# Norms before seven FFNs finished in two halves of the tokens

## What is computed

```python
def rmsnorm(x, g):
    y = xf * lax.rsqrt(jnp.mean(xf * xf, axis=-1, keepdims=True) + NORM_EPS)
    return y.astype(x.dtype) * g

def modulate(h, g, shift, scale):
    return rmsnorm(h, g) * (1 + scale) + shift

def swiglu(y, w_gu, w_down):
    gate, up = jnp.split(y @ w_gu, 2, axis=-1)
    return (jax.nn.silu(gate) * up) @ w_down

def half_ffn(h, m, off, g, w_gu, w_down):
    y = modulate(h, g, m[off], m[off + 1])
    return h + 0.5 * m[off + 2] * swiglu(y, w_gu, w_down)

...
        x = deepnorm_residual(x, f, g1, ln_g[l, 0], ln_b[l, 0], 0.5)
        u = modulate_2(x, sh2, sc2)
```

## Time and profile before

| | us |
|---|---|
| median of 3 runs | 3207.75 (3206.51 to 3209.87) |
| the profiled execution, its own time | 3206.11 |
| its span, first to last instruction | 3204.3 |
| TensorE busy | 2980.6 (93%) |
| VectorE busy | 1899.3 (59%) |
| ScalarE busy | 568.7 (18%) |
| mean granted clock of TensorE | 0.97 of full |

### The profile page before, as it was taken

How to read it: one execution, slowest core, us unless ns; L and a number is a source line. 1 busy time by engine, 2 the same in 40 slices (tenths; PEclk the granted TensorE clock), 3 DMA queues, 4 the chain that set the end, 5 groups by cost and what they waited for, 6 DMA issues and landing times.

```text
span 3204.3 us, 61066 instructions
## 1 busy us (share of the span) xinstructions
PE 2980.6 (93%) x26800; PEld 2554.4 (80%) x26800; DVE 1899.3 (59%) x3378; ACT 568.7 (18%) x1289; POOL 224.4 (7%) x363
## 2 busy tenths in 40 slices
PE   7999999977988899999989999989999989989898
PEld 6444444776777699999879999977889989967898
DVE  1777666643555487686647767745326656633674
ACT  1000001443343100100231010024111020031201
POOL 0000000431342000000000000000000000000000
PEclk8999999999999899999999999999999999998999
DMA  5668986101300456466325656633335535522452
GB/s 225 235 236 314 370 336 229 66 4 56 105 4 4 171 191 234 163 228 217 126 99 175 214 180 202 212 106 112 125 112 170 176 119 181 173 69 71 132 191 94
DMA packets 365794, 514.86 MB, mean 161 GB/s; under 512 B 11536, under 2 KB 344400, under 8 KB 357984
## 3 DMA queue, kind: packets, MB, share of 16 engines
q1 hardware_dynamic: 347824, 364.11, 34.9%
q0 software_dynamic: 17136, 144.19, 11.6%
q10 hardware_dynamic: 576, 2.75, 0.2%
HBM read 509.97 MB, written 1.05 MB: 159 GB/s over the span
## 4 chain that ended last, share of the span: by engine, by line
PE 83%; DVE 5%; DMA 5%; ACT 4%; issue 2%; POOL 1%; SPq 0%; DVEq 0%; ACTq 0%; POOLq 0%
PE PS L2487 28%; PE PS L2527 15%; PE PS L2417 7%; PE PS L588 5%; PE PS L2437 5%; PE PS L608 5%; PE PS L761 3%; PE PS L1658 2%; PE PS L1583 2%; DMA ADAW<-in_ada_rows 2%; PE PS L2538 2%; PE PS L2396 2%; DMA W<-in_ffn_w_down 1%; DVE ADAW L2723 1%; PE PS L1436 1%
## 5 line engine op out<-in xcount | busy, mean ns | idle before, releaser
L2487 PE MATMUL PS<-Y,W 128*128 128x128 f32 x4928 | 594.4, 280 | 43.4 <-ACT Y L2640 32.1
L2487 PEld LDWEIGHTS PS<-Y,W 128*128 128x128 f32 x4928 | 578.1, 196 | 48.8 <-issue 34.5
L2487 PE MATMUL PS<-Y,ARENA 128*128 128x128 f32 x3696 | 438.6, 275 | 0.0
L2487 PEld LDWEIGHTS PS<-Y,ARENA 128*128 128x128 f32 x3696 | 425.9, 192 | 0.0
L2417 PE MATMUL PS<-Y,W 128*128 128x512 f32 x704 | 304.6, 596 | 2.2 <-DVE Y L2945 2.2
L2527 PE MATMUL PS<-ARENA,W 128*128 128x128 f32 x2464 | 286.5, 275 | 7.8 <-DVE ARENA L2829 5.0
L2527 PEld LDWEIGHTS PS<-ARENA,W 128*128 128x128 f32 x2464 | 280.1, 192 | 9.7 <-DVE ARENA L2829 6.7
L2417 PEld LDWEIGHTS PS<-Y,W 128*128 128x128 f32 x704 | 134.5, 191 | 171.6 <-issue 171.1
L2723 DVE SCALAR_TENSOR_TENSOR ADAW<-ADAW,CB 128x1024 f32<-128x1024 f32 x200 | 238.6, 1221 | 29.4 <-DMA ADAW<-in_ada_rows 28.9
L608 PE MATMUL PS<-W 64*64 64x64 f32 x4608 | 116.4, 226 | 45.4 <-ACT W L858 24.5
L2437 PE MATMUL PS<-ARENA,W 128*128 128x512 f32 x352 | 154.2, 601 | 4.7 <-DVE ARENA L2777 4.7
(11 more groups left out here) (399 smaller groups left out, 3702.6 us busy)
## 6 DMA issues: line engine op xcount, KB each, us to landing
ADAW<-in_ada_rows POOLq DMA_DIRECT2D x52, 2048.0 KB, 8.8
W<-in_ffn_w_gu SPq DMA_DIRECT2D x88, 1024.0 KB, 8.0
W<-in_ffn_in SPq DMA_DIRECT2D x88, 1024.0 KB, 7.6
W<-in_ffn_w_down SPq DMA_DIRECT2D x32, 1408.0 KB, 11.2
W<-in_ffn_out SPq DMA_DIRECT2D x32, 1408.0 KB, 9.1
ADAW<-in_ada_rows POOLq DMA_DIRECT2D x64, 512.0 KB, 6.5
W<-in_even_w_in SPq DMA_DIRECT2D x40, 512.0 KB, 4.7
W<-in_e_w_in SPq DMA_DIRECT2D x22, 512.0 KB, 4.8
```

Source lines behind the costliest of these rows:

```text
L2487: last = mm(block_bank(b, q), w[left][:, k, q * P:(q + 1) * P], YB[right][:, k], start=(k == 0 and p not in (2, 5)), stop=(k == 3), skip_g ...
```

## The change

In the norms before the seven small FFNs (`by_half`), VectorE takes the reciprocal of tokens 0 to 127 alone, multiplies tiles 0 to 3 and then 4 to 7 of those tokens, and does the same with tokens 128 to 255. ScalarE scales and shifts 128 columns at a time, all eight tiles of the first half and then all eight of the second: sixteen steps for eight. `s_y` counts the first half alone, one for every second tile; a new semaphore `s_yh` counts the second half, one for every four tiles, and the token sums wait for that one.

```diff
@@ norm, deepnorm, program @@
-            add("rms", layer, 3 * k, T, n_rs, vec("norm_g", 24 * layer + 8 * k, 8), bump("y"), n["nx"])
+            add("rms", layer, 3 * k, T, n_rs, vec("norm_g", 24 * layer + 8 * k, 8), bump("y"), n["nx"], of is not None)
...
-            add("layer_norm", n_rs, g, b, then, bump("y") if then else None, n["nx"])
+            add("layer_norm", n_rs, g, b, then, bump("y") if then else None, n["nx"], of is not None)
...
@@ ScalarE @@
-            def modulated(src, layer, k, n_nx):
+            def modulated(src, layer, k, n_nx, by_half=False):
 
                 sh = MOD[:, layer, 8 * k:8 * (k + 1)] if k is not None else GS[:, 1]
+                if by_half:
+                    for h in range(2):
+                        t = slice(HT * h, HT * (h + 1))
+                        for j in range(DT):
+                            if j % 4 == 0:
+                                act.wait_ge(s_nx, n_nx - PIECES + 1 + 2 * h + j // 4)
+                            ins = A(Y[:, j, t], (Y[:, j, t] if k is not None else X[:, 0, j, t]), ACT.Identity,
+                                    bias=sh[:, j:j + 1], scale=GS[:, 0, j:j + 1])
+                            if h == 0 and j % 2 == 1:
+                                ins.then_inc(s_y, 1)
+                            if h == 1 and j % 4 == 3:
+                                ins.then_inc(s_yh, 1)
+                    return
...
@@ VectorE @@
             def token_sums(b, done, n_, n_y=None):
                 if n_y:
-                    dve.wait_ge(s_y, n_y - PIECES // 2)
+                    dve.wait_ge(s_yh, n_y - 1)
                 V.tensor_tensor(b["T1"], b["B12"], b["B11"], ALU.subtract).then_inc(done, 1)
                 dve.wait_ge(done, n_ + 1)
                 if n_y:
-                    dve.wait_ge(s_y, n_y)
+                    dve.wait_ge(s_yh, n_y)
...
-                        token_sums(YB, s_ty, 4 * i, n_y)
+                        token_sums(YB, s_ty, 4 * i, 2 * (i + 1))
...
+            def normed_by_half(dst, late=None):
+
+                for h in range(2):
+                    t = slice(HT * h, HT * (h + 1))
+                    link(V.reciprocal(RS[:, t], RS[:, t]))
+                    for i in (0, 4):
+                        if late and i:
+                            late(h)
+                        V.tensor_tensor(dst[:, i:i + 4, t], X[:, 0, i:i + 4, t],
+                                        RS[:, t].unsqueeze(1).to_broadcast([P, 4, HT]), ALU.mult).then_inc(s_nx, 1)
+
...
                 dve.wait_ge(s_rs, n_rs)
+                if by_half:
+                    normed_by_half(Y[:, :, 0:S])
+                    return
...
                 dve.wait_ge(s_rs, n_rs)
+                if by_half:
+                    normed_by_half(X[:, 0])
+                    return
```

More of the change, by code:

```diff
@@ L227, in build @@
         s_yl = sem("y_of_first_sequence_ready")
+        s_yh = sem("y_of_second_half_ready")
         s_nx = sem("normed_piece_ready")
@@ L2250, in program @@
             x_scales[bump("xa")] = (vec("final_g", 0, DT), None)
-            add("layer_norm", n_rs, vec("final_g", 0, DT), None, (2, 0), bump("y"), n["nx"])
+            add("layer_norm", n_rs, vec("final_g", 0, DT), None, (2, 0), bump("y"), n["nx"], True)
             if stop == 2:
@@ L2642, in modulated, with rms @@
                     ins.then_inc(s_y, 1)
-            def rms(layer, k, T, n_rs, g, n_y, n_nx):
+            def rms(layer, k, T, n_rs, g, n_y, n_nx, by_half):
                 if T > S:
@@ L2647, in rms, with layer_norm @@
                 else:
-                    modulated(slice(0, S), layer, k, n_nx)
-            def layer_norm(n_rs, g, b, then, n_y, n_nx):
+                    modulated(slice(0, S), layer, k, n_nx, by_half)
+            def layer_norm(n_rs, g, b, then, n_y, n_nx, by_half):
                 if then:
-                    modulated(slice(0, S), None, None, n_nx)
+                    modulated(slice(0, S), None, None, n_nx, by_half)
                     return
@@ L2929, in small_ffn, with first_rms @@
                 dve.wait_ge(s_ev, sec["t1"])
-            def first_rms(layer, k, T, n_rs, g, n_y, n_nx):
+            def first_rms(layer, k, T, n_rs, g, n_y, n_nx, by_half):
                 kt = DT // PIECES
```

## The result

| | before | after |
|---|---|---|
| median on the same chip, us | 3209.03 (3206.51 to 3214.56, 6 runs) | 3221.64 (3214.68 to 3228.41, 6 runs) |
| ratio to before, 95% interval | | 1.0039 (1.0024 to 1.0055) |
| profiled execution, own time | 3206.11 | 3221.04 |
| its span | 3204.3 | 3219.3 |
| mean granted clock | 0.97 | 0.968 |

The change makes the kernel slower, by 12.6 us in these runs. Repeated later without any edit beside 30 runs of before, it was slower by 9.8 us, ratio 1.0032 (1.0020 to 1.0044). The forecast was +9.9 and 3216.0; the 3221.64 of the first comparison lies 0.6 above the range.

A forecast was written before the change was run, and what follows sets the result against it. TensorE paces each small FFN from product 2 on, so its start and TensorE's clock count. Later product 2 (+4.1 us) and half clock (+5.8) add 9.9 to 3206.1, giving 3216.0 us, range 3208.5 to 3221.

The forecast's parts named there:

- Bound and path: Small FFN heads: product 2's start counts; product 1 comes 1.0 us sooner, off the path, as its copy follows sixteen ScalarE steps.
- ScalarE's spacing: Scale-and-shift before each small FFN: sixteen 128-column steps 0.39 us apart, 0.48 long, against eight 0.49 apart now.
- Product 2 later: Seven small FFN heads: product 2 at 8.50 us after the root's end, usually 8.15 now; +4.1 us in sum.
- Token sums: VectorE's T1 and T2 wait for the second half; 1.3 us of slack before product 6 asks, cost nothing.
- Clock: TensorE at half clock behind product 2: 1.4 us a norm, 9.8 over seven, less 4.0 now: +5.8 us (-4.0 to +7.2).
- The sum: Whole kernel: 4.1 for later product 2 plus 5.8 for half clock, +9.9 us on 3206.1, giving 3216.0.
- 1.4 for the spread: Allowance in the range's upper end of 3221 for the spread of the runs: 1.4 us.
- The clock costs what it does now: Rival: TensorE's low stretch is over by product 2, only the later copy costs: +4.1, 3210.2 us; chance 0.31.
- Cheap short steps: Rival: ScalarE's steps 0.30 us apart, product 2 up to 1.1 us sooner, total 3196 to 3200 us; chance 0.06.
- Nothing on the path: Rival: ScalarE's steps 0.36 us apart, product 2 not later, clock as now: 3206 to 3208 us; chance 0.06.

The follow-up runs named there:

- copy_dve: Changed kernel, with VectorE and not ScalarE copying product 1 in the first unit of each small FFN: 3204.32 us, ratio 0.9993 to before.
- warm_before: Kernel before the change, with 512-column matmuls nobody reads filling TensorE's pauses before products 1 and 2 of the seven norms: 3202.61 us, ratio 0.9986.
- warm_wide: Changed kernel, with 512-column matmuls nobody reads filling TensorE's pauses before products 1 and 2 in all seven norms: 3209.20 us, ratio 1.0008 to before.
- again: The changed kernel run once more without any edit, beside runs of before: 3214.36 us, ratio 1.0032.
- split: Changed kernel, with VectorE scaling and shifting tokens 128 to 255 while ScalarE does the first half alone: 3195.35 us, ratio 0.9974 to before.

## Why the prediction was right or wrong

- **Bound and path.** Right. Product 2's start is what counts, the first product came 1.0 us sooner (2.84 forecast and measured) and brought nothing, and the copy waits for nobody. copy_dve confirms it: with the copy elsewhere, all of the loss is gone. So do warm_before and warm_wide: with full clock in both, the change is still 6.6 us slower.
- **ScalarE's spacing.** Right: 0.385 us against 0.39, length 480 ns. By the Trainium skill, ScalarE: Activation LUTs, section What ACT_TABLE_LOAD costs, an estimate of 0.386 had come out, and the trace agrees with it; the nearest row of the trace would have been off by 0.09, since it has one operand less.
- **Product 2 later.** Forecast 8.50 after the root's end and +4.1 in sum, measured 8.40 and +3.35. The copy issued at 7.98, 0.08 sooner than I put it: the steps are 0.005 closer, fifteen times.
- **Token sums.** Right: T2 at 8.18, its end before product 6 asks, no cost seen.
- **Clock.** Forecast +5.8, measured +6.5 in the first profile and 7.5 - 4.1 = 3.4 in that of again. The mechanism was right in part only. The forecast had one low stretch of 3.4 us, brought by the second pause, behind every product 2, and a loss of 1.4 and at most 1.6 us a norm. In after two norms lost nothing, three lost 2.0, 2.6 and 2.7, and in three a single low stretch, in which product 1 already ran, went on unbroken for 10.2 us. Nor does it take a second pause of 2 to 3 us: copy_dve, with 0.59 us of it in the norm shown, lacks as many records. The 4.0 that the clock costs now came from one profile; four profiles with unedited heads give 1.7 to 4.1. That the sum came out near 5.8 was in part luck. And the forecast added the clock to the queue as if the two were apart, where half clock in product 1 hides a part of the queue.
- **The sum.** +9.9 forecast; the heads of the profile of after give 9.85, and the unedited repeat is 9.8 slower than before on the same chip. That these agree to 0.1 is luck: the heads of the repeat's own profile give 6.6, and the interval of its ratio reaches from 6.4 to 14.1 us.
- **The step that failed** is the last one: "1.4 for the spread". I took the 3.4 us over which three runs of before spread for the width of a measurement. Before alone spread over 11.8 us in 30 runs and after over 13.7 in six, and the mixer, which the change does not touch, alone varied by 10 us over twelve profiles. The upper end of 3221 had 1.4 for that, and 3221.64 passed it. The 3216.0 itself rested on a base of 3206.1, 2.9 below the median of the same runs of before, 3209.03; with that base the forecast is 3218.9. The remaining 2.7 us are within the interval of the ratio (7.7 to 17.6 us). So even a profile in which products 1 and 2 were well predicted does not fix the total within 5 us.
- **Rivals.** "The clock costs what it does now" would have given +4.1; it is out: 94 and 66 records are missing in the two profiles of after where four with unedited heads lack 15 to 36, and both measured differences lie above 4.1 with their whole interval. "Cheap short steps" is out at 0.385. "Nothing on the path" is out.

## What to carry to other kernels

When a consumer needs only the first part of a result, halving the producer's steps makes the first part early and all of it late: count what stands behind the producer on its own queue. Here that was a copy of 0.4 us which the next product waited for, and the fixed part of ScalarE's step, paid sixteen times, undid the 1.0 us won ahead. Move half of the steps to another engine (split), or the thing behind them (copy_dve, which brought the time back to that of before), ahead of cutting the tiles finer. Where two causes meet in one stretch, as the queue and the clock do here, count each with the other taken away, in both kernels, before giving each its share. And judge a change of 0.3% by runs on the same chip and by stages that the change touches, never by the whole of one profile.

## What the runs showed of the hardware that was not expected

- A stretch with the same instructions took 549.9 to 559.9 us in twelve profiles, at the same busy time on VectorE and ScalarE and a mean granted clock between 0.954 and 0.939. It alone is as large as the change's effect.
- After a pause of 3.35 us, short work and a second pause, the clock in the 6 us behind product 2 ranged over all there is: in after, two of seven windows at full clock, three at 0.63 to 0.72, and two at 0.52 and 0.54. Matmuls of no use in the pauses brought all seven to 1.00.
- A fetch of instructions that falls within a load of weights delays the load by about 1 us (36 loads: 10.9 to 11.6 us with it, 9.7 to 10.4 without), and whether it falls there moves with what stands ahead in the program: 30 more matmuls brought it in, 120 more took it out.
- VectorE scales and shifts eight tiles of 128 columns in 2.14 us, 0.27 each, where ScalarE takes 0.385 for each.
